# Gate tiles of an encoder layer: the sigmoid made of an exponential on ScalarE and an add and a reciprocal on VectorE

## The reference, cut to what matters

```python
n = _rmsnorm(h, norm_mix_g[i])
proj = n @ w_in[i]
q, k, v, hy, g_a, g_h = jnp.split(proj, SPLITS, axis=-1)
...
a_out = _window_attention(q, k, v, attn_sink[i])
...
h_out = _hyena(hy, hy_conv_w[i], hy_conv_b[i], kf, hy_skip[i])
merged = jax.nn.sigmoid(g_a) * (a_out @ w_attn_up[i]) + jax.nn.sigmoid(g_h) * (h_out @ w_hyena_up[i])
h = h + merged @ w_out[i]
h = h + _expert_choice(_rmsnorm(h, norm_ffn_g[i]), w_router[i], w_exp_gate[i], w_exp_up[i], w_exp_down[i])
```

## Time and profile before

| what | us |
|---|---|
| median of 3 runs | 1907.43 (1904.76 to 1908.11) |
| the profiled execution, its own time | 1907.09 |
| its span, first to last instruction | 1905.3 |
| gate tiles in the profile | about 200 to 406 |
| hyena stage | about 406 to 587 |
| experts | about 790 to 1865 |

### The profile page before, as it was taken

One profiled execution on the slowest core, in us unless ns is written; L12 is line 12 of the kernel. 1 busy time (PEld: TensorE's weight loads), 2 busy tenths in 40 slices (PEclk: granted clock), 3 DMA queues, 4 the chain that ended last, 5 costly groups with the idle time before them and its releaser, 6 DMA issues.

```text
span 1905.3 us, 25337 instructions
## 1 busy us (share of the span) xinstructions
PE 1833.4 (96%) x9378; PEld 1445.2 (76%) x9378; DVE 1410.4 (74%) x1457; ACT 1195.2 (63%) x1331; POOL 308.2 (16%) x219
## 2 busy tenths in 40 slices
PE   8999999989998999699999999999999999999996
PEld 7899777879998987477777777777777777777774
DVE  6564222138874533899999999999999999999996
ACT  5225666645553311477778777777777777777775
POOL 1224122235642600000001000100100100000010
PEclk9999999999998999799999999999999999999998
DMA  6332221192108372899999999999999999999994
GB/s 188 110 88 86 74 83 61 44 248 73 56 6 286 119 261 83 275 371 368 374 393 375 371 391 380 375 382 375 376 380 385 375 363 393 376 374 387 380 355 180
DMA packets 240187, 506.01 MB, mean 266 GB/s; under 512 B 22002, under 2 KB 56666, under 8 KB 240058
## 3 DMA queue, kind: packets, MB, share of 16 engines
q1 hardware_dynamic: 229498, 484.12, 70.6%
q0 software_dynamic: 10624, 21.03, 4.5%
HBM read 474.12 MB, written 31.28 MB: 265 GB/s over the span
## 4 chain that ended last, share of the span: by engine, by line
PE 65%; DVE 2%; issue 1%; ACT 1%; POOL 0%; POOLq 0%; DVEq 0%; ACTq 0%
PE bank L251 21%; PE bank L250 21%; PE bank L252 21%; PE bank L2271 2%; PE bank L245 1%; PE bank L2067 1%; PE bank L2053 0%; DVE w_ring L2471 0%; DVE top_values L1973 0%; DVE top_index L1975 0%; DVE affinity L1976 0%; ACT we_hi L2331 0%; DVE we_lo L2406 0%; DVE gated L1914 0%; ACT w_ring L2370 0%
## 5 line engine op out<-in xcount | busy, mean ns | idle before, releaser
L2406 DVE TENSOR_TENSOR we_lo<-w_ring,we_hi 128x2048 fp32r<-128x2048 f32 x382 | 864.9, 2288 | 68.8 <-ACT we_hi L2331 62.6
L2331 ACT ACTIVATE we_hi<-w_ring 128x2048 fp32r<-128x2048 f32 x380 | 724.3, 1914 | 97.3 <-PE bank L252 97.1
L250 PE MATMUL bank<-we_hi,gathered_turned_hi 128*100 128x512 f32 x1024 | 403.7, 394 | 1.5 <-DVE gathered_turned_lo L2410 1.5
L251 PE MATMUL bank<-we_lo,gathered_turned_hi 128*100 128x512 f32 x1024 | 403.5, 394 | 0.0
L252 PE MATMUL bank<-we_hi,gathered_turned_lo 128*100 128x512 f32 x1024 | 400.8, 391 | 0.0
L250 PEld LDWEIGHTS bank<-we_hi,gathered_turned_hi 128*100 128x100 f32 x1024 | 168.4, 164 | 67.5 <-issue 1.7
L252 PEld LDWEIGHTS bank<-we_hi,gathered_turned_lo 128*100 128x100 f32 x1024 | 168.3, 164 | 66.8
L251 PEld LDWEIGHTS bank<-we_lo,gathered_turned_hi 128*100 128x100 f32 x1024 | 168.1, 164 | 63.8
L250 PE MATMUL bank<-normed_hi,w_hi 128*128 128x400 f32 x544 | 196.5, 361 | 9.6 <-ACT u_padded L786 4.9
L250 PE MATMUL bank<-we_hi,hidden_turned_hi 128*100 128x512 f32 x512 | 203.8, 398 | 0.4 <-DVE we_lo L2406 0.4
L251 PE MATMUL bank<-we_lo,hidden_turned_hi 128*100 128x512 f32 x512 | 201.5, 394 | 0.0
(11 more groups left out here) (322 smaller groups left out, 2583.9 us busy)
## 6 DMA issues: line engine op xcount, KB each, us to landing
w_ring<-in_w_exp_gate SPq DMA_DIRECT2D x64, 2048.0 KB, 14.2
w_ring<-in_w_exp_up SPq DMA_DIRECT2D x64, 2048.0 KB, 13.7
w_ring<-in_w_exp_down SPq DMA_DIRECT2D x64, 2048.0 KB, 15.3
w_raw<-in_w_in SPq DMA_DIRECT2D x68, 256.0 KB, 4.1
gate_rows<-gate_sig SPq DMA_DIRECT2D x16, 400.0 KB, 2.6
sig_pair<-gate_rows SPq DMA_DIRECT2D x8, 800.0 KB, 5.3
hy_conv_rows<-u_conv SPq DMA_DIRECT2D x12, 400.5 KB, 3.3
w_out<-in_w_out SPq DMA_DIRECT2D x8, 512.0 KB, 8.2
```

What stands on the lines that cost most here:

```text
L250: nc.tensor.matmul(out, whi, xhi, start=first, stop=False)
L251: nc.tensor.matmul(out, whi, xlo, start=False, stop=False)
L2331: act.activation(whi[(2 * k + half) % 4][:, :], ring[k % RING][:, half * HC:(half + 1) * HC], ACT.Copy).then_inc(w_hi, 1)
L2406: nc.vector.tensor_tensor(wlo[u][:, :], ring[k % RING][:, half * HC:(half + 1) * HC], whi[u][:, :].bitcast(F32), ALU.subtract).then_inc(w_ ...
```

## The change

ACT now takes the gate tiles through `Exp` with a scale of -1, so that the buffer holds exp(-x). A new function on DVE, `gate(t)`, adds one and takes the reciprocal, both over the whole tile and in place, and counts `gated`, for which SP's store now waits in place of `taken`. DVE runs `gate` of the tile before at the start of a weigh tile, or after the masks of a scores tile, and that of the last tile after the loop.

```diff
             if kind == "gate":
-                sp.wait_ge(taken, 2 * a + 2)
                 if gt == 0:
                     sp.wait_ge(normed, ntok)
                     sp.dma_start(g.wraw[:, :, :], io["hy_filt_wout"][0].rearrange("k (q c) -> k q c", q=4)).then_inc(g.wraw_in, 16)
+                sp.wait_ge(gated, gt + 1)
                 sp.dma_start(g.sigS[gt * P:(gt + 1) * P, :].rearrange("p (a c) -> p a c", a=2), sg[gt % 2][:, :, :])\
                   .then_inc(sig_store[gt % 2], 16)
...
                 elif kind == "gate":
-                    last = act.activation(sg[gt % 2][:, k, :], b[:, 0:HALF], ACT.Sigmoid)
+                    last = act.activation(sg[gt % 2][:, k, :], b[:, 0:HALF], ACT.Exp, scale=-1.0)
...
+        def gate(t):
+            dve.wait_ge(taken, 2 * (FIRST_GATE + t) + 2)
+            nc.vector.tensor_scalar(sg[t % 2][:, :, :], sg[t % 2][:, :, :], 1.0, None, ALU.add).then_inc(one_more, 1)
+            dve.wait_ge(one_more, t + 1)
+            nc.vector.reciprocal(sg[t % 2][:, :, :], sg[t % 2][:, :, :]).then_inc(gated, 1)
+
         for gt, (slot, b) in enumerate(SLOTS_BY_TILE):
+            if gt and slot == "weigh":
+                gate(gt - 1)
...
+            if gt and slot == "scores":
+                gate(gt - 1)
...
+        gate(len(SLOTS_BY_TILE) - 1)
```

More of the change, by code:

```diff
@@ L489, in stage_mix @@
     gain_in, ones_set, gain_out, first_hi, first_lo = S("gain_in ones_set gain_out first_w_hi first_w_lo")
+    one_more, gated = S("gate_one_more gate_inverted")
     at_in, scored, masked, prep, exped, summed, divided, turned, copied, pv, o_out, at_own = S(
```

## The result

The changed kernel takes 1911.11 us (median of 11 runs, 1907.51 to 1912.52), the kernel before 1907.43 beside it. The ratio is 1.0018, with a 95% interval from 1.001 to 1.0026: slower by about 3.4 us, 2 to 5. That is within the prediction's whole range and, being under 0.2%, on the side of "no change", though with the whole interval above one. The forecast of +0.9 us was 2.5 us too low, and +3.4 lies above the range that the likeliest case had for itself, -2.2 to +2.2. The profiled run of the changed kernel has a span of 1908.8 us, 3.5 more than before, so it is a fair picture of the difference. Lines stand 1 higher than before up to the gate code and 12 higher from the hyena stage on (L791 is L792, L1611 is L1623).

What follows compares the result with a forecast made beforehand. PE was taken to set the pace nearly everywhere. Removed stalls -4.9 us and the last gate +5.8 us gave +0.9 us on 1907.09, so 1908.0, or 1908.3 against the median; range 1903.3 to 1913.2 us.

Steps and rivals of the forecast that it cites:

- the likeliest case: Whole kernel: stalls' gain of 4.9 us less 5.8 us at the last gate; 1908.3 us, own range 1905 to 1910.5, chance 0.62.
- DVE the bound: Rival, gate loop: at 6.4 us a reciprocal, late masks make PE wait; sum +4.2 us, 1911.6 us, chance 0.13.
- slow store: Rival, passage into hyena stage: last store lands in 7.3 us, nothing given back; sum +5.3 us, 1912.7 us, chance 0.08.
- the stalls are gone: Against the rival that PE's stalls stay, ACT waiting for its buffer instead of the table; +5.8 us, 1913.2 us, chance 0.05.
- the giving back: Hyena stage: DVE's 3.06 us wait for a decay table absorbs part of an 8.9 us delay, leaving 5.8 us.
- six stalls: Gate tiles: PE's waits for ACT's take, less ordinary gaps, all vanish with the table loads; 4.9 us, bounds 3.9 and 7.2.
- The add: Gate tiles, DVE: sixteen adds on 128x800, 0.57 us each.
- The reciprocal: Gate tiles, DVE: sixteen reciprocals on 128x800, 5.2 us each by the small ones' slope; ends 0.99 and 6.4.
- the rival built on it: Gate loop: DVE becomes the bound; with a reciprocal of 6.8 us the sum would be +5.5 us; chance 0.13.
- The loop: Gate loop: DVE's waits hide the new gates; copy-out about 4 us late in the shortest stretch, cost nothing.
- The last gate: Passage into hyena stage: last store leaves 5.8 us later, lands in 6, ACT starts 8.9 us later; 5.8 us stays.
- PE's clock: Passage into hyena stage: falls to 1.2 GHz before and after alike, counted at nothing; longer low clock would mean wrong altogether.

Runs made afterwards that it cites:

- experiment 3: Changed kernel without DVE's adds and reciprocals: all 16 gate tiles take the exponential, each store goes out with it; 1902.35 us, ratio 0.9975.
- experiment 1: Changed kernel, but the last gate tile goes back to a sigmoid on ACT, its store waiting for that; 1902.35 us, ratio 0.997.
- experiment 2: Kernel before, but only the last gate tile takes exponential, add and reciprocal; the other 15 keep the sigmoid; 1914.29 us, ratio 1.0041.
- experiment 4: Changed kernel, but POOL issues its four inverse-table loads only after all gate stores have landed; 1907.1 us, ratio 0.9997.
- experiment 5: Kernel before, but POOL issues its four inverse-table loads only after all gate stores have landed; 1906.15 us, ratio 0.9993.
- experiment 7: Changed kernel, but the last gate tile has its own buffer, so ACT starts the hyena stage without waiting for its store; 1907.52 us, ratio 1.0004.
- experiment 6: Changed kernel, but the last gate tile by sigmoid and POOL's four inverse-table loads after all gate stores have landed; 1901.6 us, ratio 0.9971.

## Why the prediction was right in kind and short in size

The time alone doesn't speak for the likeliest case: 1911.1 is closer to the rivals' 1911.6 (DVE the bound) and 1912.7 (slow store) than to its 1908.3, and by its own sum its range ended at 1907.43+2.2 = 1909.6; the 1910.5 written there adds the 2.2 to the forecast instead. The traces decide. DVE is not the bound in the loop, the store doesn't land in 7.3 us, and the stalls are gone; the mechanism is the likeliest case's, with the giving back too large.

**The gain.** Forecast 4.9 us from six stalls, measured 4.5 at the last take in the traces, 4.8 and 5.7 by the ratios of experiments 3 and 1. Right, and experiment 2 shows that the table loads carry it: with them the five waits are back at 7.2 us.

**The new work.** The add was forecast at 0.57 us and takes 0.51 to 0.57 in the loop, once 0.68, but 1.00 at the last tile. The reciprocal was forecast at 5.2 us and takes 5.153. The slope from one to four columns held over 800: (5153-154)/799 is 6.26 ns a column. The Trainium skill's page "VectorE: DVE Perf Modes" (section on the 8-slice pipeline in each mode) gives the reciprocal a repeat count of 8 and no time. Read as eight cycles an element that was an estimate of 6.8 us; the trace shows about six at the page's 0.96 GHz, so it doesn't bear that reading out, and the rival built on it fails.

**The loop.** Forecast at nothing, and experiments 1 and 3, with and without the gates there, can't be told apart. The tight place is where it was put. The timeline of the changed kernel at tiles 9 to 11 answers to the earlier trace rows:

```profile
328.71 5.15 DVE L1076 RECIPROCAL gate_sig<-gate_sig 128x800 f32<-128x800 f32 x1
334.55 0.68 DVE L1108 TENSOR_TENSOR wout_lo<-wout_sum_diff,wout_hi_twice 64x512 fp32r<-64x512 f32 x1
335.75 5.15 DVE L1076 RECIPROCAL gate_sig<-gate_sig 128x800 f32<-128x800 f32 x1
340.82 0.16 DVE L1000 COPY attn_out<-bank 128x64 f32<-128x64 f32 x1
341.30 0.44 DVE L970 CUSTOM_DVE_ANT_0 scores<-bank,band 128x272 f32<-128x272 f32 x1
344.24 0.44 DVE L970 CUSTOM_DVE_ANT_0 scores<-bank,band 128x272 f32<-128x272 f32 x1 [2.13 <-PE bank L656]
```

DVE runs from the first gate through the copy-out to the first mask with a single gap, of 0.16 us; by the second pair of masks it waits for PE again. PE's only wait for DVE's masks, 1.08 us at 200.96, stands before the first gate and was there before (1.07 at 200.77). ACT never waits for its buffer in the loop.

**The last gate.** ACT's start 8.9 us later after the take: measured 9.07 (12.61 less 3.54), from a store 6.23 us later and a landing 2.9 longer. Right, with a landing of 5.8 where I took 6, in part by luck: the store leaves 0.43 us later than forecast because of the add, and the landing makes up for half of that. The 6 was a choice between 2.9 and 7.3, and experiment 4 shows what made it long.

**The step that failed** is the 3.06 us that the decay wait was to give back. It gave back 1.44: the product is 7.63 us later where 5.8 was forecast. The product has a second input, a tile of taps that PE makes in a PSUM bank behind the spectra of the first split taps. Its last matmul, in the kernel before and in the changed one:

```profile
416.30 0.41 PE L1422 MATMUL bank<-wout_lo,features_hi_lo 128*128 128x256 f32 x1
420.89 0.41 PE L1434 MATMUL bank<-wout_lo,features_hi_lo 128*128 128x256 f32 x1
```

In the changed kernel the product follows its end, 421.30, by 0.14 us. Before, the same matmul ended at 416.71, so the product could have started at about 416.85, and of the wait that ended at 418.30 only 1.4 us was slack. Experiment 5 takes the decay wait away in the kernel before and finds PE there. I asked what is late next on the stage as a whole, but not which second input of the waiting instruction comes next. With 1.44 in its place the forecast would have been -4.9+7.5 = +2.6. With the measured 9.07 for 8.9 and a gain of 4.5 for 4.9 it is 3.1, the 3.14 us by which the product is late; the span is 3.5 longer, and the last 0.4 comes later and stays unexplained.

**PE's clock** was counted on neither side, and a longer time at the low clock was named as a sign of being wrong altogether. The windows of the kernel before and, behind them, of the changed kernel (PE's busy time, granted clock, DMA share, GB/s):

```profile
410.00:412.00 2.00, 0.00 (x0) 0.85 1.41 325
416.00:418.00 2.00, 2.00 (x11) 0.50 1.22 360
418.00:420.00 2.00, 0.73 (x5) 0.95 1.23 340
```

```profile
408.00:410.00 2.00, 1.15 (x5) 0.51 1.91 334
416.00:418.00 2.00, 1.11 (x5) 0.50 1.12 326
418.00:420.00 2.00, 2.00 (x10) 0.50 0.75 248
422.00:424.00 2.00, 1.16 (x10) 1.00 0.00 0
```

It is at 1.2 GHz from 408 to between 421 and 422, twice as long as before (between 411 and 412 to 418), and PE stood idle ahead of it, from 403.3 to 408.85. But on the chain only the work from 416.88 on runs at it, 5 us, where before it was that from 412.30 on, 5 to 6 us. So in these two traces the lower mean, 0.80, doesn't look like a cost of its own; no run tests it.

Between executions of one kernel the clock does go with the time. Nine of the eleven of the changed kernel have a mean granted clock of 0.981 to 0.984 and take 1910.6 to 1912.5 us; the other two have 0.986 and take 1907.5 and 1907.8. The profiled pair has 0.985 before and 0.983 after, and outside the passage the clock is low in the same places for nearly the same time. Which stretches were low in the other executions no trace shows, so how much of the 3.4 us goes with the clock stays open.

## What to carry to other kernels

Work that is free in a pipelined loop has its price at the last turn, where nothing follows to hide it: look at the passage out of the loop first, and leave the last turn as it was if the path through it gets longer (here that alone turns 3.4 us lost into 5.7 won). A stall that seems to give back time gives back only the distance to the next input of the same instruction; look that one up. A transfer on the path that leaves later may meet traffic that it used to leave ahead of, so price it by its new neighbours.

## What the hardware showed that was not expected

Some DVE operations stretch while POOL works. The add of 128x800 takes 0.51 to 0.57 us in the loop and 0.58 at the last tile with POOL idle (experiment 4), but 1.00 and 1.01 where POOL was issuing its four loads (the changed kernel, experiments 2 and 7), and 0.68 once in the loop, at 375.22, where POOL was issuing the tables for the way ahead. The reciprocal, in place as well, doesn't stretch: 5.15 us in all 16 tiles, also beside those loads. The split of 128x512 takes 0.68 us at its place in the kernel before and 2.49 to 2.50 us beside POOL's back-to-back sums (experiments 5 and 6), ending half a microsecond after the last of them. The Trainium skill's page "SBUF — State Buffer" (section "Who interferes with whom") has a rule for it: VectorE and GpSimd share a port pair, which one holds for a whole instruction while the other is blocked. The split agrees with it in kind; here DVE was held up for several POOL instructions in a row, not one. That isn't so every time: in experiment 4 the split met a row of POOL's sums at 419.70 and took 0.72 us, and it was POOL's next sum that took 1.14 in place of 0.72. That a load POOL issues slows an add fits the same rule, since moving the loads away brought the add back to 0.58 us; which part of issuing them does it, no run here tells apart.
